# Two-layer hybrid sequence block on one core: the gate products of layer 0 before its scan, four gate projections of layer 1 from the attention into the scan, ten value copies from VectorE to ScalarE

## The reference

```python
for l in range(2):
    shift, scale, gate = split(silu(c) @ w_ada[l] + b_ada[l])       # context: another vector
    h = x * (1 + scale) + shift
    if l == 0:   # even layer
        ya = rmsnorm(gla_scan both ways (q, k, v, g)) * silu(h @ w_gate)   # 4 heads, chunks of 64
        #   g = log_sigmoid(lr @ gla_gate_w + gla_gate_b) / 16 ; o = masked(q e^b, k e^-b) v + q e^b S
        yb = neighbourhood_attention(q, k, v, context, rpb) * silu(h @ w_gate)   # 8 heads
    else:        # odd layer
        yc = rmsnorm(mlstm_scan both ways (q, k, v, input gate, forget gate)) * silu(...)  # 4 heads
        yd = sliding_window_attention(rope(q), rope(k), v, context, sink) * silu(...)      # 8 heads
    x = layer_norm(ALPHA * x + gate * (concat(...) @ w_out))
```

## Time and profile before

| | us |
|---|---|
| runs of the kernel | 1599.84, 1601.24, 1605.86 (median 1601.24) |
| the profiled execution | 1599.84 |
| its span, from first to last instruction | 1598.0 |
| TensorE busy | 1515.7 (95%) |
| VectorE busy | 757.7 (47%) |
| ScalarE busy | 570.3 (36%) |
| GpSimd busy | 35.8 (2%) |

### The profile page before, as it was taken

One profiled execution on the slowest core, in us unless ns is written; L12 is line 12 of the kernel. 1 busy time (PEld: TensorE's weight loads), 2 busy tenths in 40 slices (PEclk: granted clock), 3 DMA queues, 4 the chain that ended last, 5 costly groups with the idle time before them and its releaser, 6 DMA issues. The chain is left out here.

```text
span 1598.0 us, 25566 instructions
## 1 busy us (share of the span) xinstructions
PE 1515.7 (95%) x9656; PEld 1037.7 (65%) x9656; DVE 757.7 (47%) x1653; ACT 570.3 (36%) x1320; POOL 35.8 (2%) x108
## 2 busy tenths in 40 slices
PE   7999989899899999898999999999999999999996
PEld 4665876577467577555588866478574555556985
DVE  3144555423221322332577756255554555665776
ACT  0134364533332422442202342223334555564033
POOL 0000000000000000000000000000000010011000
PEclk9999999999999999999999999999999999999999
DMA  9200020240421422400234511222220200001543
GB/s 378 96 27 27 2 103 21 81 157 28 167 83 60 148 70 95 166 14 27 106 132 151 197 66 65 70 67 63 57 80 29 104 14 14 14 27 36 171 160 123
DMA packets 72037, 139.80 MB, mean 87 GB/s; under 512 B 6656, under 2 KB 44588, under 8 KB 70572
## 3 DMA queue, kind: packets, MB, share of 16 engines
q1 hardware_dynamic: 66604, 135.55, 24.7%
q10 hardware_dynamic: 5312, 2.62, 0.6%
HBM read 125.43 MB, written 12.71 MB: 86 GB/s over the span
## 5 line engine op out<-in xcount | busy, mean ns | idle before, releaser
L1251 PE MATMUL proj<-hT,weights 128*128 128x512 f32 (+1 forms) x752 | 315.7, 565 | 4.8 <-DMA weights<-in_weights 2.2
L1251 PE MATMUL mixed<-hT,weights 128*128 128x512 f32 (+1 forms) x672 | 257.8, 532 | 1.1 <-DMA weights<-in_weights 1.1
L1251 PEld LDWEIGHTS proj<-hT,weights 128*128 128x128 f32 x752 | 137.7, 191 | 133.8 <-issue 128.0
L1251 PEld LDWEIGHTS mixed<-hT,weights 128*128 128x128 f32 x672 | 125.6, 194 | 98.5 <-issue 91.1
L2086 ACT ACTIVATE work<-turned 128x512 f32<-128x512 f32 (+2 forms) x136 | 72.7, 535 | 146.3 <-PE turned L1341 106.3
L1789 DVE TENSOR_TENSOR yT<-turned,work 128x128 f32<-128x128 f32 x72 | 21.0, 292 | 159.6 <-PE turned L1359 135.0
L2086 ACT ACTIVATE work<-work,stat 128x640 f32<-128x640 f32 (+8 forms) x98 | 74.0, 755 | 31.5 <-DVE stat L1760 29.5
L1341 PE MATMUL turned<-consts,work 128*128 128x128 f32 (+3 forms) x448 | 69.2, 283 | 10.9 <-DVE yT L1789 8.6
L1341 PEld LDWEIGHTS turned<-consts,work 128*128 128x128 f32 (+3 forms) x448 | 48.7, 139 | 43.3 <-issue 19.1
L1235 PE MATMUL mixed<-weights,hT 128*128 128x256 f32 x320 | 71.5, 380 | 0.0
L1235 PEld LDWEIGHTS mixed<-weights,hT 128*128 128x128 f32 x320 | 60.1, 190 | 8.8 <-issue 1.0
(11 more groups left out here) (343 smaller groups left out, 2586.6 us busy)
## 6 DMA issues: line engine op xcount, KB each, us to landing
weights<-in_weights SPq DMA_DIRECT2D x130, 512.0 KB, 4.0
tables<-in_bias SPq DMA_DIRECT2D x8, 1281.0 KB, 6.3
pair<-in_weights SPq DMA_DIRECT2D x20, 512.0 KB, 7.0
hT<-in_xT SPq DMA_DIRECT2D x8, 640.0 KB, 16.4
yT<-in_weights SPq DMA_DIRECT2D x8, 512.0 KB, 8.9
work<-in_xT SPq DMA_DIRECT2D x16, 256.0 KB, 2.7
x1T<-yT SPq DMA_DIRECT2D x8, 512.0 KB, 3.0
work<-rows SPq DMA_DIRECT2D x32, 128.0 KB, 3.4
```

The source lines that it names most:

```text
L1251: last = nc.tensor.matmul(PJ[BANK_OF[u]][:, 0:n], weights[:, w % WBUFS, k, :], src[:, k, t0:t0 + n], start=(k == 0), stop=(k == KT - 1))
```

## The change

In four places the steps stand elsewhere or on another engine. The diff, cut:

```diff
@@ make_schedule, layer 0
-    s += between(values("gla", 0), [("gate0", x, None) for x in range(6)])
+    s += between(values("gla", 0), [("gate0", x) for x in range(len(GATE_UNITS))])
...
-    s += scans(0, [between(qkv("gla", 1), [("gate0", x, Slot()) for x in range(6, 12)]), na_v, ...
+    s += scans(0, [qkv("gla", 1), na_v, ...
@@ make_schedule, layer 1
-    first = k[:4] + g[8] + k[4:8] + g[9] + k[8:] + v
+    first = k[:4] + g[8] + k[4:8] + g[9] + k[8:] + v[:4] + g[10] + v[4:12] + g[11] + v[12:]
-    third = vv[:4] + g[13] + vv[4:8] + g[10] + vv[8:] + g[11] + rq[0][:5] + g[14] + rq[0][5:] + g[15]
+    third = vv[:4] + g[13] + vv[4:8] + g[14] + vv[8:] + g[15] + rq[0][:5] + g[0] + rq[0][5:] + g[1] + g[2] + g[3]
-    last = attention(1, [rq[1] + g[0], rq[2] + g[2], rq[3] + g[4], g[5] + g[7]], [g[1], g[3], g[6]])
+    last = attention(1, [rq[1], rq[2], rq[3], gates[7]], gates[4:7])
@@ TensorE
-            def s_gate0(x, u):
+            def s_gate0(x):
-                if u is not None:
-                    wait_bank(pe, u)
-                elif x >= 2:
+                if x >= 2:
                     pe.wait_ge(*at(("g", x - 2)))
...
             def s_lin_chunk(q, n):
-                    pe.wait_ge(*at(("g", 5)))
+                    pe.wait_ge(*at(("g", len(GATE_UNITS) - 1)))
@@ VectorE, s_mm
-                elif dest == "vt":
+                elif dest == "vt" and kind[0] == "gla":
@@ ScalarE, s_mm
-                if dest in ("vv", "vt"):
+                if dest == "vv" or dest == "vt" and kind[0] == "gla":
                     return
                 act.wait_ge(*at(("proj", u)))
+                if dest == "vt":
+                    prev = pair_slot(kind)[1]
+                    for r in readers(prev) if prev and t0 == 0 else []:
+                        act.wait_ge(*at(r))
+                    run(value_tiles(kind, t0), two_tiles(u), ACT.Copy,
+                        [("proj_free", u)] + ([("filled", *kind)] if t0 + n == T else []))
+                    return
```

More of the change, by code:

```diff
@@ L448, in make_schedule @@
     s += [("early_copy",)] + project(("lr",), "lr", CHUNKS_ALL)
-    s += between(values("gla", 0), [("gate0", x, None) for x in range(6)])
+    s += between(values("gla", 0), [("gate0", x) for x in range(len(GATE_UNITS))])
     na = qkv("na", 0)
     na_v = [x for x in na if x[1] == ("na", 0, "v")]
-    s += scans(0, [between(qkv("gla", 1), [("gate0", x, Slot()) for x in range(6, 12)]), na_v, between([x for x in na if x not in na_v], ada(0, range(16, 24))) + [("vgather", 0)]])
+    s += scans(0, [qkv("gla", 1), na_v, between([x for x in na if x not in na_v], ada(0, range(16, 24))) + [("vgather", 0)]])
     gates = [project(("gate", 0, f), "gate", [c]) for f in range(8) for c in CHUNKS_ALL]
@@ L509, in make_schedule @@
             continue
-        at = {"mm": 5, "ada": 3, "ada_turn": 3, "lin_turn": 2, "rows_turn": 2, "gate0": 2, "gates": 3, "gates_sum": 3, "fast": 5}.get(st[0])
+        at = {"mm": 5, "ada": 3, "ada_turn": 3, "lin_turn": 2, "rows_turn": 2, "gates": 3, "gates_sum": 3, "fast": 5}.get(st[0])
         if at is not None and st[at] is not None:
@@ L797, in gate_sums @@
             return yT[:, 4 + 2 * d + p, :]
-        def gate_bank(x, u):
-            return (SC[:, x % 2 * 512:x % 2 * 512 + 512] if u is None else PJ[BANK_OF[u]])[:, 0:CHUNKS_ALL[GATE_UNITS[x][0]][1]]
         def gate_unit(t, d, p):
@@ L1377, in s_gate0 @@
                 (t0, n), o = CHUNKS_ALL[ci], (2 * d + p) * P
-                done(nc.tensor.matmul(gate_bank(x, u), gate_w[0:97, o:o + P], kvT[0:97, t0:t0 + n], start=True, stop=True),
-                     ("gate", x))
+                done(nc.tensor.matmul(SC[:, x % 2 * 512:x % 2 * 512 + n], gate_w[0:97, o:o + P], kvT[0:97, t0:t0 + n],
+                                      start=True, stop=True), ("gate", x))
             def s_ml_keys(q):
@@ L1798, in s_gate0 @@
                 g = gate_sums(d, p)[:, t0:t0 + n]
-                link(V.scalar_tensor_tensor(out=g, in0=gate_bank(x, u), scalar=0.0,
-                                            in1=gate_temp[x % 2][:, 0:n], op0=ALU.min, op1=ALU.subtract), ("g", x),
-                     *([("proj_free", u)] if u is not None else []))
+                link(V.scalar_tensor_tensor(out=g, in0=SC[:, x % 2 * 512:x % 2 * 512 + n], scalar=0.0,
+                                            in1=gate_temp[x % 2][:, 0:n], op0=ALU.min, op1=ALU.subtract), ("g", x))
                 if d:
@@ L2211, in s_gate0 @@
                 na = gate_temp[x % 2][:, 0:n]
-                run(na, gate_bank(x, u), ACT.Abs)
+                run(na, SC[:, x % 2 * 512:x % 2 * 512 + n], ACT.Abs)
                 run(na, na, ACT.Exp, scale=-1.0)
```

## The result

The changed kernel takes 1614.28 us in the median of 14 runs (1607.53 to 1619.15), the kernel before 1601.93 (1599.72 to 1607.57) on the same chips: the ratio is 1.0072, 95% interval 1.0054 to 1.0089, some 11.6 us slower. Against the 1601.24 that the prediction was made from that is 1612.8. The forecast was 1607.5 in a range of 1594 to 1614, with 0.54 for "no change" and 0.34 for "slower". So the range held it, by 1.2 us, the likeliest bracket didn't, and the forecast was 5.3 us too low.

A forecast was written before the change was run, and what follows sets the result against it. TensorE, busy 1515.7 of 1598.0 us, was taken as the bound, so only its waits count. Terms +5.1 - 4.0 - 1.5 + 4.0 + 2.0 + 2.4 - 1.7 = +6.3 on 1599.84 gave 1606.1, 1607.5 as a median; range 1594 to 1614.

The forecast's parts named there:

- no change: Bracket for the whole kernel's time: within 8.0 us (0.5 per cent), 1593.2 to 1609.2 us; chance 0.54.
- part 1: Layer 0's values: all 12 decay gates there make third products and the scan's first product wait, +5.1 us.
- part 2: Layer 0's scan: without gates its waits go, less one new bank wait, -4.0 us; gain bounds 2.5 and 5.6.
- part 3: Rows chain: with value copies on ScalarE it starts earlier and TensorE waits less at its end, -1.5 us.
- part 4: First fill of layer 1's scan: two chunks in one bank wait for ScalarE's copy behind its squares, +4.0 us.
- part 5: Third fill of layer 1's scan: norm waits go (-2.5), three meetings in one bank come (+4.5), +2.0 us.
- part 6: Layer 1's attention: losing four gates exposes waits, two old waits go, +2.4 us; bounds -2.4 and +8.
- clock: Slow 1.2 GHz stretches (falls) behind TensorE's waits: -3.4 for old ones lost, +1.7 for new, -1.7 us.
- rival B: Layer 1's attention bound by latency wherever a part was lost, +8 there: 1613.1 us; chance 0.23 together with rival A.
- rival A: Clock falls behind the new waits, clock term +5.1 instead of -1.7: 1614.3 us; chance 0.23 together with rival B.
- my own signs of being wrong: Long-run wait under 1.5 us, attention's window shrinking over 27 or under 22 us, or slow clock stretches adding up to more.
- my own case: The whole kernel: the forecast sum with its own spread, 1603 to 1611 us; chance 0.45.

The follow-up runs named there:

- e5: The changed kernel with layer 1's scan banks given out by last use instead of first use: 1598.02 us, ratio 0.9981 to the kernel before.
- e2: The kernel before with only layer 1's ten value copies moved from VectorE to ScalarE: 1597.74 us, ratio 0.9977.
- e4: The changed kernel with layer 0's decay gates left where they were: 1611.74 us, ratio 1.0060 to the kernel before.
- e10: e9 with banks by last use in layer 0's scan too: 1586.39 us, ratio 0.9916 to the kernel before.
- e7: The kernel before with two output gates moved from the attention into the first fill of layer 1's scan: 1606.13 us, ratio 1.0038.
- e8: The kernel before with layer 1's value copies on ScalarE and layer 0's decay gates spread singly between its values: 1590.98 us, ratio 0.9934.
- e9: e8 with layer 1's scan banks given out by last use: 1587.77 us, ratio 0.9919 to the kernel before.

## Why the prediction was right and where it was wrong

Forecast beside measured, in us:

| step | forecast | measured |
|---|---|---|
| part 1, three gates in a row, twice | +4.4 | +4.2 (2.09 each) |
| part 1, scan's first product | +0.7 | +0.1 |
| part 2, waits of layer 0's scan | -4.0 | -4.0 (part 1 and the stage's +0.3) |
| part 3, rows chain | -1.5 | -1.5 (0.9 of it at another wait) |
| part 4, long run of values | +4.0 | +4.3 |
| part 5, third fill | +2.0 | +2.0 (4.9 new, 2.9 gone) |
| part 6, attention | +2.4 | +3.1 to +4.1 (3.6 here) |
| clock | -1.7 | +3.1 in the profile, +3.0 ±2.1 over all runs |

The mechanism, waits of TensorE each at its place, was right in parts 1, 2, 4 and 5; the table's waits sum to +9 where I had +8, and all runs without falls give +9.4. The rule of the Trainium skill that spoke against the change ("Perfetto Trace Analysis", section "Matmuls": groups should rotate through banks) agrees with that: 9.2 of the 15 us that e5 regains are waits at meetings in one bank.

In part 3 the 1.5 us are right, but by a cause that I had only by half: the chain ends earlier as forecast, TensorE's wait at its end hardly shrinks, and an earlier wait of 0.93 goes. Part 6 was short by about 1 us (0.7 to 1.7), and its terms aren't borne out singly: of the two waits that I let go, the 1.0 for L1778 is still 0.9. The waits there rose from 14.0 to 16.8 in all, close to the forecast, and the rest is outside the waits that the profile names. In part 1 the wait at the scan's first product was 2.62 and not 3.2.

The bounds of two parts don't follow from their terms: part 2's come out as 2.0 and 4.8 from my own rows, not 2.5 and 5.6, and part 6's upper one is 6.2 with the 2.4 taken off or 8.6 without, not 8. Only rival B's time rests on one of them.

The step that failed is the clock, "I take -3.4 and +1.7". I paired falls with waits: the ones behind 2.79, 3.14 and 1.74 "lose their cause". In fact falls came behind the new waits at 114 and 1118 and behind one of 2.62, and the fall behind the rows chain stayed, since the wait there is 2.86 and not the 1.6 that I gave it. One came inside the attention, at 1448.9, where I had counted none. It is not a function of the wait either. Behind the same 2.86 us e2's profile has no fall, though the changed kernel's has. e4 has the old wait at layer 0's first scan product, as long as in the earlier trace rows, and a fall behind it that the kernel before hasn't:

```profile
114.50:117.90 3.40, 3.40 (x21) 1.82 (x22) 1.33 (x4) 2.57 (x8) 0.00 (x0) 0.50 0.01 2
```

So rival A was partly right; its price, +5.1, is more than the profile's +3.1. Over all runs the clock is +3.0 and the rest +9.4. That the clock costs more in the changed kernel is measured; why, the runs don't show. Of my own signs of being wrong one came true, the slow stretches adding up to more than before; the attention's window, 22.2 us shorter, came close to another, and its fall makes 1.7 of that. That the range held the time is in part luck: its upper end was the time of rival A, not of my own case.

The chances followed from that: with the clock at +3 in place of -1.7 the same sum is 1612.3, beyond the bound of 1609.2.

## What to carry to other kernels

Look at where a bank was used last, not at where it was first given out: an order that puts two chunks into one bank back to back stops TensorE for the copy and for all that stands ahead of the copy in its engine's queue. Where an order moves work in front of a shared half-buffer, count how many users come in a row, and spread them. Take the falls of the clock as a term with a spread, not as a debit of single waits, and take them out of every run by its mean granted clock before comparing kernels.

## What of the hardware was not expected

The time at the 1.2 GHz level differs from one execution to the next by more than these kernels' waits do. The 71 runs of the kernel before have mean granted clocks of 0.985 to 0.993, which is 24 to 11 us lost, with the same program. Their times have a standard deviation of 3.2 us; with the loss taken out it is 1.5. The profiles are single draws of this: 23.0 us at the slow clock in e10's, 46.5 in e7's, 45.3 in e8's, 29.4 in e9's (whose waits sum to only 0.8 us less than e8's), and 33.4 in that of the kernel before. At half its length the stretch from 23.0 to 46.5 is 12 us, as much as the whole effect of this change. Single profiles can't tell such kernels apart by their length; the medians of many runs can, and the times without falls can better.
